# The sums of a chunked state-space scan with channels on the partitions, in a four-layer backbone

## The reference, cut to what matters

```python
def step(h, inp):                       # one chunk of 128 tokens
    xc, dtc, bc, cc = inp
    cum = jnp.cumsum(dtc * a, axis=1)
    seg = cum[:, :, None, :] - cum[:, None, :, :]
    decay = jnp.exp(jnp.where(lower[None, :, :, None], seg, -jnp.inf))
    xdt = xc * dtc[..., None]
    scores = jnp.einsum('blhn,bshn->blsh', cc, bc) * decay
    y = jnp.einsum('blsh,bshp->blhp', scores, xdt)
    y = y + jnp.einsum('blhn,bhpn->blhp', cc * jnp.exp(cum)[..., None], h)
    tail = jnp.exp(cum[:, -1:, :] - cum)
    h_new = h * jnp.exp(cum[:, -1, :])[:, :, None, None] + \
        jnp.einsum('bshn,bshp->bhpn', bc * tail[..., None], xdt)
    return h_new, y
...
y = (y_f + flip(y_b_rev)).astype(xs.dtype) + xs * d_skip[:, None]
return _rms_norm(y.reshape(...) * jax.nn.silu(z), norm_g) @ w_out
```

## Time and profile before

| | |
|---|---|
| three timed runs | 1496.92, 1497.04, 1500.73 us |
| the profiled execution: its time, its span | 1496.32 us, 1495.1 us |
| busy share of the span | PE 95%, PEld 78%, DVE 75%, ACT 46%, POOL 21% |
| chain that ended last, by engine | PE 73%, DVE 16%, issue 3%, DMA 3%, ACT 3%, POOL 1% |
| mean granted PE clock | 0.985 |
| DMA | 201.05 MB, mean 134 GB/s |

### The profile page before, as it was taken

The page is one execution under the profiler, slowest core; times in us unless marked ns, Lnnn a source line. Parts: engine busy times, 40 slices in busy tenths (PEclk is TensorE's granted clock), DMA queues, the critical chain, the costliest instruction groups (busy, mean ns, idle before and its releaser), DMA issues.

```text
span 1495.1 us, 22099 instructions
## 1 busy us (share of the span) xinstructions
PE 1422.5 (95%) x8313; PEld 1171.4 (78%) x8313; DVE 1114.4 (75%) x1688; ACT 685.7 (46%) x1201; POOL 314.7 (21%) x381
## 2 busy tenths in 40 slices
PE   4899999999989999999899999999999999999987
PEld 2787888888877889776578787787888788888865
DVE  0699999999995477767658655556338999899896
ACT  1555555455542353545544332233324656555652
POOL 0044344443441011001001000000001333334340
PEclk8899999999999999999899999999999999999999
DMA  9246644556444412324332437435340444434433
GB/s 349 68 140 170 197 129 131 164 169 197 133 145 141 133 47 85 114 82 170 116 120 79 154 114 226 140 113 171 119 125 20 117 128 126 114 113 133 141 115 134
DMA packets 133690, 201.05 MB, mean 134 GB/s; under 512 B 9872, under 2 KB 102736, under 8 KB 133584
## 3 DMA queue, kind: packets, MB, share of 16 engines
q1 hardware_dynamic: 121616, 163.08, 34.1%
q0 software_dynamic: 10304, 33.86, 8.4%
q10 hardware_dynamic: 1664, 2.70, 0.5%
HBM read 198.26 MB, written 1.34 MB: 134 GB/s over the span
## 4 chain that ended last, share of the span: by engine, by line
PE 73%; DVE 16%; issue 3%; DMA 3%; ACT 3%; SPq 1%; POOL 1%; DVEq 0%; ACTq 0%
PE ps L458 19%; PE ps L460 19%; PE ps L459 19%; PE ps L489 2%; PE ps L641 2%; PE ps L647 2%; DVE w_lo L427 2%; DVE xc L943 2%; PE ps L2022 1%; PE ps L2006 1%; DVE ylo L1515 1%; PE ps L600 1%; DVE stats L1813 1%; PE ps L633 1%; PE ps L632 1%
## 5 line engine op out<-in xcount | busy, mean ns | idle before, releaser
L458 PE MATMUL ps<-h_hi,w_hi 128*128 128x512 f32 (+2 forms) x1088 | 412.0, 379 | 7.8 <-issue 5.2
L459 PE MATMUL ps<-h_lo,w_hi 128*128 128x512 f32 (+2 forms) x1088 | 398.6, 366 | 0.0
L460 PE MATMUL ps<-h_hi,w_lo 128*128 128x512 f32 (+2 forms) x1088 | 398.6, 366 | 0.0
L427 DVE TENSOR_TENSOR w_lo<-raw,w_hi 128x1024 fp32r<-128x1024 f32 (+1 forms) x203 | 249.4, 1244 | 137.1 <-ACT w_hi L418 136.0
L418 ACT ACTIVATE w_hi<-raw 128x1024 fp32r<-128x1024 f32 (+1 forms) x203 | 207.1, 1051 | 167.6 <-PE ps L460 124.9
L458 PEld LDWEIGHTS ps<-h_hi,w_hi 128*128 128x128 f32 (+1 forms) x1088 | 205.4, 189 | 50.7 <-issue 12.1
L460 PEld LDWEIGHTS ps<-h_hi,w_lo 128*128 128x128 f32 (+1 forms) x1088 | 205.4, 189 | 33.9
L459 PEld LDWEIGHTS ps<-h_lo,w_hi 128*128 128x128 f32 (+1 forms) x1088 | 205.6, 189 | 30.9
L943 DVE SCALAR_TENSOR_TENSOR xc<-ps,gp,xc 128x508 f32<-128x508 f32 (+1 forms) x224 | 161.3, 723 | 13.6 <-ACT xc L780 10.7
L460 PE MATMUL ps<-w_hi,ylo 128*128 128x512 f32 x376 | 149.2, 397 | 0.0
L1212 POOL DMA_DIRECT2D cum_b<-cum_scratch x96 | 71.8, 754 | 261.3 <-PE ps L641 175.4
(11 more groups left out here) (263 smaller groups left out, 2509.6 us busy)
## 6 DMA issues: line engine op xcount, KB each, us to landing
raw<-in_mod_w SPq DMA_DIRECT2D x80, 512.0 KB, 4.5
raw<-in_ssm_w_in SPq DMA_DIRECT2D x64, 512.0 KB, 6.1
cum_b<-cum_scratch POOLq DMA_DIRECT2D x96, 256.0 KB, 6.3
raw<-in_ssm_w_in SPq DMA_DIRECT2D x66, 256.0 KB, 4.2
raw<-in_ssm_w_out SPq DMA_DIRECT2D x32, 512.0 KB, 4.7
raw<-in_pool_w_in SPq DMA_DIRECT2D x32, 512.0 KB, 4.7
raw<-in_attn_w_in SPq DMA_DIRECT2D x20, 512.0 KB, 3.7
raw<-in_pool_w_out SPq DMA_DIRECT2D x16, 512.0 KB, 4.3
```

Source lines behind the costliest of these rows:

```text
L427: dve.tensor_tensor(lo, w_shaped(key, raw[:, r % RS, :], width), hi.bitcast(F32), ALU.subtract).then_inc(lo_done, 1)
L458: pe.matmul(o, hi_s, hi_m, start=first, stop=False)
L459: pe.matmul(o, hi_s, lo_m, start=False, stop=False)
L460: return pe.matmul(o, lo_s, hi_m, start=False, stop=last)
```

## The change

The sums of the scan are formed with the channels on the partitions and the tokens along the columns, which is how `ys` holds them, so that they need no turning.

- `pe_intra` swaps its operands: x is stationary (64 columns of one head), the weights move (128 columns), and heads alternate between the output partitions 0 to 63 and 64 to 127. `pe_inter` swaps too: two halves of a state are stationary and C moves.
- `pe_turn_y` is gone. The gate reads `y` in SBUF in place of PSUM, and stands at another place of DVE's list: one half behind `offset(0)`, one behind `least(0)`.
- The factor exp(cum) varies along the columns now. It is written to DRAM once a layer (four more DMAs of ACT) and loaded as a broadcast to `ec` for each group, by two DMAs of POOL's queue (`ssd_pool_ec`).
- D times x reads the SiLU of x, which now goes to `ys`, and is two operations with a scale per partition; `z_silu` therefore waits for it, and it waits for the gate of the group before.
- `xw` has two buffers in place of three: `weighted(2)` waits for `pe_states` 0 of its own group, and stands in POOL's list behind `forward_part(0)`, `(1)` and the `ec` loads, ahead of D times x, `forward_part(2)`, `(3)` and the squares.
- `cum_b` is loaded with one DMA a chunk in place of two. `pe_states` 1 and 2 don't wait for the gate any more. Some small buffers share memory, with waits to match (a first SiLU, `act_gate`, the late weight units).

```diff
     def pe_intra(pe, L, g, c0, b):
...
             for h in range(HG):
-                o = bank[b][:, GW * (c - c0) + PH * h:GW * (c - c0) + PH * h + PH]
-                last = pe.matmul(o, cum_b[:, c, 0, h, :], xT[:, c, PH * h:PH * h + PH], start=True, stop=True)
+                t, e = divmod(h, 2)
+                q = SEG * t + 128 * (c - c0)
+                last = pe.matmul(bank[b][PH * e:PH * e + PH, q:q + 128], xT[:, c, PH * h:PH * h + PH],
+                                 cum_b[:, c, 0, h, :], start=True, stop=True)
...
     def pe_inter(pe, L, g, b, *states):
         s = lay[L]
         for a, (c, k, d) in enumerate(states):
-            last = pe.matmul(bank[b][:, GW * a:GW * a + GW], c_of(g)[:, 128 * c:128 * c + 128],
-                             Hs[:, k, d, :], start=True, stop=True)
+            for t in range(2):
+                q = SEG * t + 128 * a
+                last = pe.matmul(bank[b][:, q:q + 128], Hs[:, k, d, 128 * t:128 * t + 128],
+                                 c_of(g)[:, 128 * c:128 * c + 128], start=True, stop=True)
...
         def z_silu(n, t):
             act.wait_ge(s["z_p"], 3 * n + 1 + 2 * t)
+            act.wait_ge(s["dx_g"], 2 * n + t + 1)
...
+        def gate(o, t):
+            if t == 0:
+                dve.wait_ge(s["y_d"], y_done(L, o, "c3"))
+            dve.wait_ge(s["z_a"], 2 * o + t + 1)
+            dve.tensor_tensor(ys[:, 2 * o + t, t0:], y[:, t, t0:], ys[:, 2 * o + t, t0:],
+                              ALU.mult).then_inc(s["g0_d"], 1)
...
-        decay(0)
+        offset(0)
+        if i >= 2:
+            gate(i - 2, 0)
+        least(0)
+        if i >= 2:
+            gate(i - 2, 1)
...
         def weighted(k):
...
-            if g:
-                pool.wait_ge(s["st_p"], 3 * (g - 1) + k + 1)
+            if k == 2:
+                pool.wait_ge(s["st_p"], 3 * g + 1)
+            elif g:
+                pool.wait_ge(s["st_p"], 3 * (g - 1) + (3, 2)[k])
...
         pool.wait_ge(s["turned_a"], 3 * g + 2)
-        for k in range(3):
-            weighted(k)
+        weighted(0)
+        weighted(1)
         forward_part(0)
         forward_part(1)
-        if g:
-            pool.wait_ge(s["yt_p"], 2 * g)
-        for c in range(first, NT):
-            last = pool.tensor_tensor(y[:, c, :].rearrange("p (h q) -> p h q", q=PH),
-                                      xT[:, c, :].rearrange("p (h q) -> p h q", q=PH),
-                                      spread(sg[:, g, 128:132], PH), ALU.mult)
-        last.then_inc(s["dx_g"], 1)
+        ssd_pool_ec(pool, L, g)
+        weighted(2)
+        for t in range(2):
+            if g:
+                pool.wait_ge(s["g0_d"], 2 * (g - 1) + t + 1)
+            pool.tensor_scalar(y[:, t, t0:], ys[:, 2 * g + t, t0:], dskc[:, 2 * g + t:2 * g + t + 1], None,
+                               ALU.mult).then_inc(s["dx_g"], 1)
         for n in range(2, nc):
             forward_part(n)
```

More of the change, by code:

```diff
@@ L408, in w_place_free @@
         elif key in IS_LATE:
-            eng.wait_ge(lay[key[0]]["x_p"], 3)
+            eng.wait_ge(lay[key[0]]["t1_p"], 4 * GRP)
         elif RING_OF[key] >= WS:
@@ L607, in pe_turn_inputs @@
         last.then_inc(s["t1_p"], 1)
[L609 to L619, removed]
     def pe_states(pe, L, g, k):
@@ L774, in first_tap @@
             else:
-                if g >= 0:
-                    act.wait_ge(s["t1_p"], 4 * g + (4 if k == 2 else k + 1))
+                if g >= 0 and k == 2:
+                    act.wait_ge(s["t1_p"], 4 * g + 4)
                 dst, a = xc[:, k, :], 0
@@ L828, in ssd_act_step @@
         if not has_in and last_layer(L):
+            turned()
             z_silu(g, 0)
-            turned()
             z_silu(g, 1)
@@ L1067, in ssd_dve_step @@
             masks()
-            gate(i - 2)
             for c in (0, 1):
@@ L1088, in ssd_dve_step @@
             y_lat(g)
-            gate(g)
+            gate(g, 0)
+            gate(g, 1)
             for c in range(6, 12):
@@ L1150, in ssd_dve_step @@
         tap(0, 3)
-        if i >= 2:
-            gate(i - 2)
         tap(1, 0)
@@ L1208, in ssd_pool_cum, with ssd_pool_ec @@
                 pool.wait_ge(s["scan_p"], scan_done(L, g - 1, "in01" if c < 2 else "in23"))
-            for d in range(2):
-                r0 = HEADS * d + HG * g
-                src = cum_dram[r0:r0 + HG, 128 * c:128 * c + 128].partition_broadcast(128)
-                pool.dma_start(cum_b[:, c, d, :, :], src).then_inc(s["cum_loaded"][c], 16)
+            src = cum_dram[g].rearrange("d h n -> (d h) n")[:, 128 * c:128 * c + 128]
+            pool.dma_start(cum_b[:, c, :, :, :].rearrange("p d h n -> p (d h) n"),
+                           src.partition_broadcast(128)).then_inc(s["cum_loaded"][c], 16)
+    def ssd_pool_ec(pool, L, g):
+        s = lay[L]
+        a = 1 if last_layer(L) else 0
+        if g:
+            pool.wait_ge(s["y_d"], y_done(L, g - 1, "m"))
+        else:
+            pool.wait_ge(ec_stored, 64 * (L // 3) + 64)
+        for e in range(2):
+            src = ec_dram.rearrange("(g t e) a n -> g e t (a n)", t=2, e=2)[g][e][:, SEG * a:]
+            pool.dma_start(ec[PH * e:PH * e + PH, :, a:, :].rearrange("p t a n -> p t (a n)"),
+                           src.partition_broadcast(PH)).then_inc(ec_loaded, 16)
     def ssd_pool_step(pool, L, g):
@@ L1330, in ssd_act_start @@
         act.wait_ge(s["dtpar_loaded"], 48)
-        act.activation(alog_b[:, :], alog_b[:, :], ACT.Exp).then_inc(s["dt_a"], 1)
+        act.activation(alog_b, alog_b, ACT.Exp).then_inc(s["dt_a"], 1)
         act_split2(act, L, "bc", 0)
@@ L1389, in ssd_dve_start @@
         dve.wait_ge(s["dtpar_loaded"], 48)
-        op("v", dve.tensor_tensor(q4(v), q4(bank[5][:, 0:256]), b4(dtb_b[:, :]), ALU.add))
+        for odd in range(2):
+            h = slice(PH * odd, PH * odd + PH)
+            dve.tensor_copy(dskc[h, :].unsqueeze(2), dsk_b[h, :].rearrange("p (n e) -> p n e", e=2)[:, :, odd:odd + 1])
+        op("v", dve.tensor_tensor(q4(v), q4(bank[5][:, 0:256]), b4(dtb_b), ALU.add))
         need("v")
```

147 lines of the change are left out of this document (75 added, 72 removed).

## The result

The changed kernel takes 1538.39 us (median of four runs, 1537.73 to 1538.84) against 1497.91 us (1496.92 to 1500.73) for the kernel before on the same chip: 1.0278 times as long, 95% interval 1.0261 to 1.0294. The direction was forecast, the size was not: +40.5 us in place of +19, and outside the range.

The account below looks back on a forecast made before the run. PE was taken to bound the kernel, with DVE's bound 0.3 us apart in layer 0 and DVE's chain setting layer 3. Layer 0 +8, layer 3 +11, ends 0: +19 on 1495.1, plus 1.9, gives 1516 us; range 1483 to 1531.

Parts of the forecast that it names:

- PE's savings: PE in the scans: turning gone, weights times x cheaper; 2.3 us a step in layer 0, 1.15 in layer 3.
- The start of tap 0 and the path behind the last mix: Layer 0 step starting at S: DVE's tap 0 of x tile 1 at S+8.6; PE's path 8.96 - 0.71 us.
- POOL resumes at S+13.9 behind the states: Layer 0 step starting at S: POOL stands still at `weighted(2)` for states 0 until S+13.9.
- S+23.5 with the turns: Layer 0 step from S: POOL's first addition of squares, S+20 at least, S+23.5 if POOL and DVE alternate over SBUF.
- the sum of layer 0: Layer 0 step: 42.3 us plus DVE's waits for POOL, 48.0, with late masks 48.4; +8 us over six steps.
- W: Layer 0 step: DVE's waits for POOL where both read SBUF, between S+13.5 and S+23 from step start S; 5.7 us.
- the strict form: Rival, chance 0.15: DVE and POOL exclude each other for whole SBUF instructions; 6.4 us waits, late masks 1.5; 1530 us.
- 5.7 + 0.4: Layer 0 step: 5.7 us of DVE's waits for POOL plus 0.4 us for later masks holding ACT's first tap.
- the formula: Layer 0 step: 8.6 + (28.4 - 3.1) + DVE's waits for POOL + 0.1 + (8.96 - 0.71), in us.
- 0.8 of 6.4: Layer 0: a DVE wait is 0.8 of the POOL operation waited for, taking the 6.4 us to about 5.7.
- D times x at 0.75 us for 512 columns, bound 1.04: POOL, each of two operations: 0.75 us taken between 0.58 and 1.04; 1.5 us a step, layer 3 0.8 to 1.2.
- The ends, counted as 0: Outside steps 2 to 7: start +1 us, layer 0's last gate about 1 us earlier, first steps unchanged; together 0.

Follow-up runs that it names:

- e4: The changed kernel with ACT making the exponentials ahead of the squares, POOL's list unchanged: 1504.2 us, 1.0064 of the kernel before.
- e2: The changed kernel with POOL adding the squares directly behind `weighted(2)`, ahead of D times x and the forward parts: 1502.6 us, 1.0047 of the kernel before.
- e12_forward_first: The changed kernel with POOL making forward parts 2 and 3 ahead of `weighted(2)`, nothing else: 1530.0 us, 1.0226 of the kernel before.

## Why the prediction was wrong in its size

- **PE's savings**: right. The old turning is gone, weights times x cost 1.02 to 1.10 us for eight where 1.02 was forecast; the states' part 2.0 to 2.3 us where 1.75 was, some 0.3 too little.
- **The start of tap 0 and the path behind the last mix**: right (S+8.7 for S+8.6; 8.20 us for 8.25), the second in part by luck. The forecast put the weights times x of both chunks behind the last mix; the matmuls of the first start ahead of it (323.58), which takes some 0.5 us off, and the states' part takes about as much more than before.
- **POOL resumes at S+13.9 behind the states**: right, S+14.2.
- **The first addition at "S+23.5 with the turns"**: S+23.95, right by luck. The forecast had 4.7 us of POOL's own work ahead of it and 4.9 us of turns; of the 9.7 us measured 6.4 are the operations at their quickest (D times x alone 3.1, not 1.5), and 3.3 what they lost. This number had no term in the sum of layer 0, and that is the step that failed. From the start of that addition to the mix there are 4.1 us more (addition 1.28, square 0.63, table load 1.28, one exponential 0.64, and the gaps), all of them in the earlier trace rows but the table load, which I hadn't looked for. The mix can't start before S+28.0.
- **W, "DVE's waits for POOL", 5.7 us (6.4 by the strict form)**: wrong in kind. DVE's stretch was 1.1 us. Its loss was 6.1 us of standing still for the exponentials. These two can't be added as forecast: had DVE lost 5.7 us to turns it would have come to the mix at about S+27, and the exponentials, by the forecast's own S+23.5 and the 4.1 us behind it, would have been ready at S+27.6. It came at S+22.1, with 0.8 us of turns behind it, and waited until S+28. That 1.1 + 6.1 lies near the 5.7 + 0.4 of the forecast is luck in the size, and so is it that the strict form's +3.1 us a step was nearly met (+3.0). Put into the formula the measured losses give 42.3 + 1.1 + 6.1 = 49.5 against 50.0 measured and 48.4 forecast. With the chain cut it gives 46.2 for 46.6 measured (work moved into the wait) and 45.4 for 46.0 (squares early), but 45.2 for 46.3 and 44.3 for 46.1 with the exponentials first: up to 1.8 us there have no term, and no run shows what they are. The 32 to 33 us that `e4` and `e2` gave back, with more stretch and not less, show which of the two it was. The recorded working also has a slip: 0.8 of 6.4 is 5.1 and not 5.7, and by it the forecast would have been some 4 us lower, farther from the result.
- **D times x at 0.75 us for 512 columns, bound 1.04**: wrong, and the mis-sized term of layer 3. The operation takes at the least 0.91 us over 256 columns and 1.56 over 512. In the changed kernel its mean is 2.08 us over 512 in layer 0 and 1.81 over 256 in layer 3, and beside other work of DVE it reached 3.58. I had priced it by operations of another kind, and under the middle of their range. In layer 3 the forecast had 2.2 us for `weighted(2)` and D times x together; they took 5.76, the first addition came 4.3 us later and not 1 to 2.7, and the step lost 3.2 us and not 1.8. Moving this one operation to ACT gives back the whole 40.5 us, though a step of layer 3 stays 0.6 us over the kernel before and one of layer 0 is 0.4 under it.
- **The Trainium skill** says in its GPSIMD Engine Reference, section Engine selection, that one-input elementwise work runs roughly at line rate on GpSimd. Here the one-input form with a scale per partition is the slower: 0.91 us against 0.61 for two operands over the same 256 columns. The measurement decides. The strict rule of its page SBUF — State Buffer, section Who interferes with whom, was in the prediction as a rival; by that section the operation that was issued second waits, on either engine. The rows agree with it in kind. The 6.4 us that the prediction worked out as DVE's share weren't there in the changed kernel: ahead of the first addition POOL lost 3.3 us, and DVE 1.1 in the whole step.
- **The ends, counted as 0**: +4.9 us. +2.2 in the first step of layer 0, +4.9 behind the two scans, and -2.2 in the start and the first step of layer 3. What the part behind the scans is isn't shown: with D times x on ACT the stretch between the scans was 761.2 us in one kernel and 768.2 in another, against 766.1 in the changed kernel. The first step stayed at 48.7 to 51.1 us in every version of the changed kernel; I didn't try what sets it.
- **Layer 3 with the chain cut** stays at 34.5 to 34.9 us, over the 33.9 of before, though PE has less to do. DVE's stretch there is 2.1 to 3.4 us where it was 0.3; `weighted(2)` now lies beside a weight split and an offset. That this is the cause of the last 0.6 us and more is argued from the rows; no run took it away.

## What to carry to other kernels

When an operation is moved behind a wait on an in-order queue, don't sum only what it costs the engine that it holds up by running beside it: follow everything behind it in that queue to whoever waits for it, through the next engine's list, to the time at which the bounding engine needs it, and put that time in the sum as a bound of its own. Two things that can make the same engine late at the same point (a stretch of its work ahead of it, a wait for another there) are a maximum and not a sum, and an edit that shrinks one shows the other. An operation whose form no row shows should be given the upper bound or more when it stands on such a chain, or be put on an engine with a row for it.

## What the runs showed of the hardware

- GpSimd's `tensor_scalar` with a scale per partition: 0.91 us at the least for 128x256, 1.56 us for 128x512, while `tensor_tensor` with the same scale as a broadcast operand takes 0.61 for 128x256 and 1.03 for 128x512 where it is quickest. ACT does the 128x512 in 0.71.
- Which engine pays, and how much, where GpSimd and DVE both read SBUF changes with what stands beside what. The two D times x operations took 3.12 us (1.56 each) where DVE stood still or read mostly PSUM; in the changed kernel they took 4.14, and DVE's 1.22 us offset beside them 1.62; in `e12_forward_first` they took 6.52, and DVE's 1.22 us split beside them 1.55.
- A GpSimd DMA issue of 512 KB takes 0.90 us against 0.75 for 256 KB, so one for two saves 0.6 us of its time.
